# Hybrid mixer and expert block: gates by Tanh, attention turns half a projection later, a gather that comes out turned, and short products in the waits of the routing

## The reference, cut to what matters

```
h = rms_norm(x, g_mix);  proj = h @ w_in            # 1024 -> 9232 columns
q,k,v = silu(causal_conv4(proj[q,k,v]))             # DeltaNet mixer, 8 heads, chunks
oa = rms_norm(gated_delta_rule(q,k,v,beta,g)) * silu(z)
p = softmax(qd . kd * scale + bias)  (2 maps per head, causal)
od = rms_norm((p0 - lam * p1) @ vd) * (1 - lam_init) # differential attention, 8 heads
x = x + (sigmoid(gate_a) * oa + sigmoid(gate_b) * od) @ w_o
h2 = rms_norm(x, g_ffn); top 4 of 32 experts by softmax(h2 @ w_router)
x = x + sum over chosen experts: w * (clamped_swiglu(h2 @ w_up[e]) @ w_down[e])
```

## Time and profile before

| | us |
|---|---|
| median of 3 runs (1353.07 to 1355.45) | 1353.12 |
| profiled execution, its own time | 1349.63 |
| its span, from the first to the last instruction | 1347.6 |
| PE busy in the span | 1253.5 |
| DVE busy | 370.1 |
| ACT busy | 255.0 |
| POOL busy | 63.6 |

### The profile page before, as it was taken

One profiled execution on the slowest core, in us unless ns is written; L12 is line 12 of the kernel. 1 busy time (PEld: TensorE's weight loads), 2 busy tenths in 40 slices (PEclk: granted clock), 3 DMA queues, 4 the chain that ended last, 5 costly groups with the idle time before them and its releaser, 6 DMA issues.

```text
span 1347.6 us, 14033 instructions
## 1 busy us (share of the span) xinstructions
PE 1253.5 (93%) x5565; PEld 542.0 (40%) x5565; DVE 370.1 (27%) x891; ACT 255.0 (19%) x517; POOL 63.6 (5%) x104
## 2 busy tenths in 40 slices
PE   6989999978998999999999999989999998999997
PEld 5878456634443333333333333323333332333332
DVE  4586734554413121121112111111211111121111
ACT  2441021355121111111111111111111111111110
POOL 5160200001000000000000000000000000000000
PEclk9999999988997999999999999999999999999999
DMA  8642533113298999999999999999999999999995
GB/s 259 144 165 84 170 109 125 63 62 119 69 398 333 429 428 427 427 427 427 427 427 427 428 427 428 428 428 427 427 427 428 427 427 428 427 428 427 428 427 216
DMA packets 57403, 452.71 MB, mean 336 GB/s; under 512 B 10713, under 2 KB 10857, under 8 KB 32673
## 3 DMA queue, kind: packets, MB, share of 16 engines
q1 hardware_dynamic: 53536, 447.76, 80.0%
q0 software_dynamic: 1488, 3.85, 1.7%
q10 hardware_dynamic: 2320, 0.26, 0.2%
HBM read 448.69 MB, written 3.15 MB: 335 GB/s over the span
## 4 chain that ended last, share of the span: by engine, by line
PE 56%; DMA 33%; DVE 7%; ACT 2%; issue 2%; SPq 0%; DVEq 0%; ACTq 0%
DMA ring<-in_w_up_dram 32%; PE pb L1420 15%; PE pb L1456 11%; PE pb L1166 7%; PE pb L1147 5%; PE pb L1375 3%; PE pb L1389 3%; PE pb L1308 2%; PE pb L1135 2%; PE pb L1381 1%; PE pb L1439 1%; DMA ring<-in_w_in_dram 1%; DVE ring L877 1%; DVE ring L876 1%; DVE ring L787 1%
## 5 line engine op out<-in xcount | busy, mean ns | idle before, releaser
L1420 PE MATMUL pb<-ring,buf_a 128*64 128x512 f32 x2048 | 456.0, 596 | 44.6 <-DMA ring<-in_w_up_dram 44.6
L1420 PEld LDWEIGHTS pb<-ring,buf_a 128*64 128x64 f32 x2048 | 143.5, 137 | 339.2 <-issue 246.6
L1456 PE MATMUL pb<-ring,buf_b 128*64 128x512 f32 x1024 | 226.8, 595 | 0.0
L1098 DVE TENSOR_SCALAR buf_a<-pb 128x512 f32<-128x512 f32 x32 | 22.1, 692 | 673.8 <-PE pb L1420 673.8
L1166 PE MATMUL pb<-ring,hT 128*128 128x512 f32 x384 | 176.6, 607 | 0.9 <-PE pb L1166 0.6
L1456 PEld LDWEIGHTS pb<-ring,buf_b 128*64 128x64 f32 x1024 | 70.7, 137 | 131.8 <-issue 127.9
L724 ACT ACTIVATE buf_a<-buf_a 128x512 f32<-128x512 f32 x32 | 20.1, 630 | 471.9 <-DVE buf_a L1098 471.9
L1166 PEld LDWEIGHTS pb<-ring,hT 128*128 128x128 f32 x384 | 71.2, 194 | 81.3 <-issue 80.7
L1147 PE MATMUL pb<-hT,ring 128*128 128x256 f32 x384 | 91.3, 393 | 2.0 <-DMA ring<-in_w_in_dram 2.0
L1147 PEld LDWEIGHTS pb<-hT,ring 128*128 128x128 f32 x384 | 74.0, 196 | 12.3 <-issue 2.4
L1375 PE MATMUL pb<-xt,buf_c 128*64 128x512 f32 x264 | 65.7, 619 | 1.0 <-DVE buf_c L1043 1.0
(11 more groups left out here) (274 smaller groups left out, 823.0 us busy)
## 6 DMA issues: line engine op xcount, KB each, us to landing
ring<-in_w_up_dram SPq DMA_DIRECT2D x128, 2048.0 KB, 41.1
ring<-in_w_down_dram SPq DMA_DIRECT2D x64, 2048.0 KB, 43.4
ring<-in_w_in_dram SPq DMA_DIRECT2D x18, 2048.0 KB, 7.9
ring<-in_w_o_dram SPq DMA_DIRECT2D x2, 2048.0 KB, 8.6
t_rows<-ring POOLq DMA_DIRECT2D x1, 1536.0 KB, 34.8
xt<-in_x_dram SPq DMA_DIRECT2D x2, 512.0 KB, 4.5
ring<-t_rows POOLq DMA_DIRECT2D x1, 1024.0 KB, 6.1
out_dram<-xt SPq DMA_DIRECT2D x2, 512.0 KB, 2.7
```

The source lines that it names most:

```text
L1420: ins = mm(pb[64 * hf:64 * hf + 64, n_, :], xg[:, c, :], slot(s)[:, at_:at_ + 512], start=False, stop=(c == KC - 1), skip_group_check=True)
L1456: ins = mm(pb[64 * hf:64 * hf + 64, 2, :], actT[:, j, hf_in, :], slot(s)[:, at_:at_ + 512], start=(c == 0), stop=(c == KC - 1), skip_group ...
```

## The change

1. **Tanh for Sigmoid in the front end.** sigmoid(v) = (1 + tanh(v/2)) / 2. The convolution's taps are halved once (`par`), SiLU is (tanh + 1) * acc in one `scalar_tensor_tensor`; the gates are (tanh + 1) * value, and the halves go into `gz` (times 0.25) and `gsubr` (times 0.5). ScalarE's table loads between Exp and Sigmoid are no longer in its stream. The expert loop keeps Sigmoid.
2. **Attention.** A step `aw` (VectorE's weights) stands at 22 + 2h, the turn `a2` at 23 + 2h and `a3` at 24 + 2h; ScalarE's copy of the turned weights (`take_turned_weights`) is no step of its own, but stands inside the take of the projection in front of the turn. Logits of the two maps alternate. ScalarE's two copies of a head's output become one. `odn` moves from 38 to 39.
3. **Early slabs.** Slabs 0 to 2 are sent behind pieces 14, 15 and 16, slabs 3 to 5 behind piece 17, ahead of the two pieces of w_o; the others as before.
4. **Routing.** `turn(1, 0)` stands inside the last `w_o_half`, `route(1, 0)` behind it. `awake(n)` issues n products of 96 x 512 bf16 that nobody reads. The first gather is `gather_turned`: 16 products of x1's columns with `sel` give the tokens turned, VectorE takes them directly. `gates` treats both token blocks at once, and stands ahead of the plan.

```diff
+    EARLY = {14: (0,), 15: (1,), 16: (2,), 17: (3, 4, 5)}
+    NEARLY = 6
...
         put(20 + 2 * h, ("a1", h))
-        put(22 + 2 * h, ("a2", h))
-        put(23 + 2 * h, ("a3", h))
+        put(22 + 2 * h, ("aw", h))
+        put(23 + 2 * h, ("a2", h))
+        put(24 + 2 * h, ("a3", h))
...
-                if RING[i] == 0:
+                if RING[i] <= 2:
                     sp.wait_ge(s_psAf, nA[("o1",)] + 1)
...
                 sp.dma_start(piece_at(n), w_piece(n)).then_inc(s_piece[n % 3], 16)
+                for s in EARLY.get(n, ()):
+                    front_dead(s)
+                    load(s)
...
-            for s in range(NSLOT):
+            for s in range(NEARLY, NSLOT):
...
-                sc.activation(sg[:, t % 3, :], acc[:, t % 3, :], ACT.Sigmoid).then_inc(s_sig, 1)
+                sc.activation(sg[:, t % 3, :], acc[:, t % 3, :], ACT.Tanh).then_inc(s_sig, 1)
...
+            def take_turned_weights(h):
+
+                act_e.wait_ge(s_atr, h + 1)
+                if h >= 2:
+                    act_e.wait_ge(s_od, h - 1)
+                sc.copy(aT[h % 2], pb[:, 6, 0:3 * P].rearrange("p (k q) -> p k q", k=3)).then_inc(s_aT, 1)
...
                     act_e.wait_ge(s_pj, 24 + q + 1)
+                    turned = [t for t in after.get(2 * q + 1, []) if t[0] == "a2"]
+                    for t in turned:
+                        take_turned_weights(t[1])
...
-                            sc.activation(tmpg[i % 2], src, ACT.Sigmoid)
+                            sc.activation(tmpg[i % 2], src, ACT.Tanh, scale=0.5)
...
-                v.tensor_tensor(silu_out(t), tok2(acc[:, t % 3, :]), tok2(sg[:, t % 3, :]), ALU.mult).then_inc(s_silu, 1)
+                v.scalar_tensor_tensor(out=silu_out(t), in0=tok2(sg[:, t % 3, :]), scalar=1.0, in1=tok2(acc[:, t % 3, :]), op0=ALU.add, op1=ALU.mult).then_inc(s_silu, 1)
...
+                    if b and n_ and c == 4:
+                        turn(1, 0)
...
+            def awake(n, bank=2):
+
+                for _ in range(n):
+                    mm(pb[:, bank, :], ones_b[0:96, :], bup3[0:96, 0:512], start=True, stop=True)
...
             w_o_half(1, 1)
+            route(1, 0)
             pe.wait_ge(s_wo, 4)
             pe.sem_inc(s_used, 1)
-            turn(1, 0)
             turn(1, 1)
-            route(1, 0)
+            awake(4)
             route(1, 1)
 
+            awake(8)
             pe.wait_ge(s_cho, NB)
...
+            def gather_turned():
+
+                for c in range(KC):
+                    rows = slice(2 * P * (c // 2) + c % 2, 2 * P * (c // 2) + 2 * P, 2)
+                    at_ = (2 * (c % 4) + c // 4) * SLOTS
+                    for b in range(NB):
+                        ins = mm(pb[:, 3, at_:at_ + SLOTS], xt[:, b, rows], sel[:, b, :], start=(b == 0), stop=(b == NB - 1))
+                return ins
+
             pe.wait_ge(s_sel, 1)
-            gather()
+            gather_turned().then_inc(s_gath, 1)
```

More of the change, by code:

```diff
@@ L670, in _ @@
                         sc.activation(junk[:, (h % 2) * 256 + b * P:(h % 2) * 256 + (b + 1) * P], src, ACT.Square, accum_out=odss[:, b, h:h + 1])
-                        last = sc.copy(OD_h[:, b, h], src)
-                    last.then_inc(s_ode, 1)
+                    sc.copy(OD_h[:, :, h], pb[:, 7, 256 * (h % 2):256 * (h % 2) + 256].rearrange("p (b j) -> p b j", b=NB)).then_inc(s_ode, 1)
             def mix_taken(b, n_):
@@ L711, in take_rows @@
                 sc.copy(xgt, pb[:, 3, :]).then_inc(s_xgt, 1)
[L713 to L714 removed]
+            act_e.sem_inc(s_xgt, 1)
             act_e.wait_ge(s_gtt, 1)
@@ L1049, in _ @@
             select(slice(0, 1))
+            v.tensor_copy(selE[:, :], seleye[:, 0:1].to_broadcast([96, SLOTS])).then_inc(s_sele, 1)
+            gates()
+            dve.wait_ge(s_zero, 1)
+            v.tensor_copy(selg[:, :, 0:E], gat)
+            v.tensor_copy(selg[:, :, 64:64 + E], gat).then_inc(s_gpad, 1)
             link(v.tensor_reduce(maxc, pb[:, 0, 128:160], AX_X, ALU.max))
@@ L1263, in _ @@
                         pe.wait_ge(s_nm, h)
+                    rows = [slice(64 * m, 64 * m + 64) for m in range(2)]
                     for m in range(2):
-                        rows = slice(64 * m, 64 * m + 64)
-                        mm(pb[:, 4 + m, 0:T], atq[rows, h, P:T], atk[rows, h, :], start=True, stop=True)
-                        ins = mm(pb[:, 4 + m, T:T + P], atq[rows, h, 0:P], atk[rows, h, 0:P], start=True, stop=True)
+                        mm(pb[:, 4 + m, 0:T], atq[rows[m], h, P:T], atk[rows[m], h, :], start=True, stop=True)
+                    for m in range(2):
+                        ins = mm(pb[:, 4 + m, T:T + P], atq[rows[m], h, 0:P], atk[rows[m], h, 0:P], start=True, stop=True)
                     ins.then_inc(s_lg, 1)
```

88 lines of the change are left out of this document (38 added, 50 removed).

## The result

| | before | after |
|---|---|---|
| median, us | 1353.36 (4 runs, 1353.07 to 1355.45) | 1329.39 (4 runs, 1328.50 to 1331.09) |
| profiled execution, its own time | 1349.63 | 1329.46 |
| its span | 1347.6 | 1327.7 |
| issue of the eleventh slab load | 432.91 | 413.18 |

The ratio is 0.9835, with a 95% interval of 0.9813 to 0.9858. The forecast was 1334 us in a range of 1326 to 1341.

The account below looks back on a forecast made before the run. The slab transfer stream, started by the eleventh load, was taken as the bound. Attention 14.1, convolution 1.0 and routing 3.7 sum to 18.8 us off the profiled execution; with 3.5 us up to the median, 1334 us, range 1326 to 1341.

Parts of the forecast that it names:

- The bound: Expert loop: transfers at 427 GB/s set the pace; the end is the eleventh slab load plus 894 us plus an unchanged tail.
- The attention: Attention stage: old waits and low clock go, less new waits, plus faster logits; 14.1 us gained, bounds 7 to 20.
- the new waits: Attention in its new order: TensorE still waits near the mixer's norm and under GpSimd's gain product, 5.9 us in all.
- The logits' 1.6 us: Attention: alternating the two maps' logits pairs the array's halves and saves 0.2 us at each of 8 heads.
- my 18.4 us: Attention before the change: 12.2 us of TensorE's waits on VectorE's weights plus 6.2 us of lower clock behind them.
- The convolution: Convolution stage: one table load of 1.28 us leaves TensorE's path; 1.0 us gained, bounds 0 and 3.3.
- the stretch under GpSimd: Convolution: during GpSimd's 4.12 us subtraction one VectorE product takes 4.17 us, and an earlier VectorE meets it all the same.
- Routing: From gather to slab 0's use: 9.7 us instead of 13.7 if short products hold the clock; 3.7 us gained after 0.3 lost.
- a clock that stays low: Rival in routing: short fillers fail to hold the clock, routing gives 0 to -2 us, time 1338 to 1340; chance 0.12.
- The early slabs: Six slab loads ahead of the output-weight pieces: no gain by themselves, bounds zero and 3 us lost.
- The slower rival: Attention: late weights delay every head through a ring of waits; about 1378 us, turning point at 2.3 us per head; chance 0.04.
- the other 4.7: The gains outside attention, convolution 1.0 us and routing 3.7 us, counted against the slower rival's losses.

Follow-up runs that it names:

- e7: The changed kernel with each head's four logits products in their old order, both of one map, then both of the other; 1327.9 us (1 run).
- e12: e10 with Sigmoid and its table loads back in the convolution alone, the gates keeping Tanh; 1324.63 us (4 runs).
- e10: The changed kernel with GpSimd's b_up splitting in quarters, the old gather by rows, copy and turn, and no last three short products; 1321.84 us (5 runs).
- e3: The changed kernel without its 19 short products that nobody reads; 1335.24 us (4 runs).
- e9: The changed kernel with GpSimd's splitting of b_up cut into quarters, each released by VectorE's progress; 1327.32 us (4 runs).
- e11: e10 with the mixer's norm at 37 instead of 28 and seven unread products ahead of tile 7's norm sums; 1320.93 us (6 runs).
- c1_changed: The changed kernel itself, unaltered, timed and profiled again; 1330.73 us (6 runs).

## Why the prediction was right, and which terms were not

**The bound** held in all 14 profiles: 914.4 to 914.7 us from the eleventh load to the end, whatever stood in front.

**The attention** gave 17.2 us, not 14.1. The step that missed is the new waits: 5.9 us in my carrying on, 1.9 by the trace (0.4 at the turn under GpSimd for my 2.0; 1.2 and 0.3 at the outputs for my 2.9 and 1.0). The pattern was right, at the norm and under GpSimd, and every size was too big. The logits' 1.6 us were wrong in kind (e7). The two errors partly cancel: 4.0 us too many for new waits, 1.6 too many for the logits. The cost before was a little more than my 18.4 us: 19.6 by waits and clock, as above (6.8 us of low clock for my 6.2, and 0.6 us on ScalarE that I had left out).

**The convolution** gave -0.1 us in this pair of profiles and not 1.0, which is less than the stage scatters, so the term is not refuted. Its working was incomplete: I had named one load on TensorE's path and there are two, 2.7 us in all, and I had named the stretch under GpSimd as what would meet an earlier VectorE, and taken less than it took: all of it. e12 and e10 show what the part is worth without it.

**Routing** gave 3.56 us for 3.7, from the cause named (the granted clock). From the gather to the eleventh load it is 9.97 us for my 9.7, in front of it 0.2 us were lost for my 0.3. But the sum hid a step of the wrong sign: it priced the turned gather rightly (3.9 us, measured 3.95) and never the old one at the same clock, against which it costs 1.0 us, and the last three short products cost 0.6. The chance of 0.12 for a clock that stays low was for a real case; e3 is that case without the fillers, at 2.5 us slower than before in this stage.

**The early slabs** gave nothing, as said.

**The slower rival** has its turning point wrong. By its own price, a wait and 2 us of low clock at each of eight heads, 23.1 us (18.4 and the other 4.7) are used up at a wait of 0.9 us a head, not of 2.3; that is 13.5 us from a head's logits to its weights, which my rows gave under GpSimd. At one head only did a wait of that size come (1.2 us).

**From the span to the median.** The sum came to 18.8 us against 19.9 in the spans. The rest of the 4.6 us between forecast and median is the 3.5 us by which the median of before lay above its profiled execution: I took the same for after, and there it was nothing. The time of a run goes with its mean granted clock, in 23 runs of the kernel before from 1344.16 us at 0.990 to 1358.72 at 0.983. The kernel before scatters over 14.6 us in these 23 runs, the changed one over 6.5 in ten (1328.50 to 1334.97), e10 over 2.0 in five. That shorter waits make the time steadier isn't shown by that: more runs scatter wider, and e9 and e11, which wait less than the changed kernel, scatter over 7.6 us in four runs and 5.5 in six. Which stage a longer run lost its time in no timed run shows.

## What to carry to other kernels

Find the one event that starts the saturated stream (here the first reuse of a ring slot) and cost every edit by what it does to that event; an edit that only hands time to the next wait is worth little until that wait is gone too. In a serial stretch where TensorE has little to do, unread products in the waits can be worth more than a shorter path, but they must not outlast the wait. Long GpSimd operations beside a VectorE that has slack per tile should be cut into pieces that fit this slack, each released by VectorE's own progress.

## What the runs showed of the hardware that I had not expected

- The clock fell behind no idle time: from 1.00 to 0.57 in 32 to 40 us of e9, with TensorE busy for the whole of the 8 us before, and not in e10 with the same code. And it fell or not behind the same wait in two profiles of one and the same kernel: the norm sums wait 1.55 us for the decay's exponentials in both, and the next tile takes 3.70 us in the changed kernel's first profile and 5.39 in c1_changed. The Trainium skill (TensorE: Matmul & The Clock Gate, "What's actually happening") says that the monitor runs free of the kernel's start, so that the same code can meet it at another phase; these two pairs agree with it, and don't prove it.
- 32 records that load 128 columns and move 64 take 3.95 us at full clock, 8 records that move 512 take 1.94, for the same gather: 2.0 us for a way that saves a copy and a turn, which together cost 1.3 (0.58 and 0.74).
- Alternating the two row halves of the array between products that write different banks gave 0.01 us of 0.86; the order of one map after the other ran side by side already.
